# A 1-core fp32 transformer kernel: two matmuls per split product instead of three, down projections in two passes, four-block sums

## The reference

```python
# first block, D_FF = 2752
x = x + 0.5 * swiglu(rms_norm(x, ffn1_norm), w_gate, w_up, w_down)
u = rms_norm(x, mix_norm) @ w_in
x = x + concat([fourier_mixer(u[:, :512]), gqa_attention(q, k, v)]) @ w_out
x = x + 0.5 * swiglu(rms_norm(x, ffn2_norm), w_gate, w_up, w_down)
x = rms_norm(x, final_norm)
# second stack, D_FF = 2816
x = x + short_conv_mixer(rms_norm(x), w_in, w_conv, w_out)
x = x + mem_cross_attention(rms_norm(x), mem_n, w_q, w_kv, w_o)
x = x + swiglu(rms_norm(x), w_gu, w_down)
x = x + moba_attention(rms_norm(x), w_q, w_o, ..., shared_kv(x))
x = x + mem_cross_attention(rms_norm(x), ...)
x = x + swiglu(rms_norm(x), w_gu, w_down)
return rms_norm(x)
```

## Time and profile before

| | |
|---|---|
| median of 3 runs | 1349.37 us (1345.59, 1349.37, 1350.83) |
| profiled execution: span from first to last instruction | 1344.9 us |
| its own time | not listed apart; the nearest run is 1345.59 us |
| TensorE matmuls busy | 1296.3 us, 96%, 10402 records |
| weight loads busy | 1277.9 us, 95% |
| VectorE, ScalarE, POOL busy | 823.6, 588.4, 117.2 us |
| mean granted TensorE clock | 0.984 of full speed |
| read from HBM | 218.47 MB, 163 GB/s over the span |

### The profile page before, as it was taken

One profiled execution on the slowest core, in us unless ns is written; L12 is line 12 of the kernel. 1 busy time (PEld: TensorE's weight loads), 2 busy tenths in 40 slices (PEclk: granted clock), 3 DMA queues, 4 the chain that ended last, 5 costly groups with the idle time before them and its releaser, 6 DMA issues.

```text
span 1344.9 us, 25191 instructions
## 1 busy us (share of the span) xinstructions
PE 1296.3 (96%) x10402; PEld 1277.9 (95%) x10402; DVE 823.6 (61%) x1137; ACT 588.4 (44%) x717; POOL 117.2 (9%) x67
## 2 busy tenths in 40 slices
PE   7999999999999999999999999998999999999997
PEld 7999999889999999999999999998999999999997
DVE  7766745666666746876555666556966546566633
ACT  6544433454444434344434444443445335444432
POOL 2100002002000000002002000016621001100000
PEclk9999998999999999999998999999999999999998
DMA  8555643234555653554344555544444344455540
GB/s 312 200 187 188 219 156 125 67 122 157 175 177 183 221 183 107 187 177 157 126 152 142 179 185 188 207 141 154 131 142 169 132 148 141 172 176 175 201 167 32
DMA packets 33540, 220.53 MB, mean 164 GB/s; under 512 B 3616, under 2 KB 4928, under 8 KB 7488
## 3 DMA queue, kind: packets, MB, share of 16 engines
q1 hardware_dynamic: 33328, 219.46, 47.8%
q10 hardware_dynamic: 144, 0.07, 0.0%
HBM read 218.47 MB, written 1.05 MB: 163 GB/s over the span
## 4 chain that ended last, share of the span: by engine, by line
PE 87%; POOL 6%; DVE 3%; ACT 2%; issue 1%; DMA 0%; SPq 0%; POOLq 0%; DVEq 0%; ACTq 0%
PE bank L366 27%; PE bank L368 27%; PE bank L367 27%; POOL work L355 4%; PE bank L581 2%; PE bank L545 1%; PE bank L426 1%; ACT work L718 1%; DVE w_lo L933 1%; POOL q_t L344 1%; DVE x L955 1%; PE bank L563 0%; ACT xn_hi L714 0%; PE bank L436 0%; POOL q_t L347 0%
## 5 line engine op out<-in xcount | busy, mean ns | idle before, releaser
L705 ACT ACTIVATE w_hi<-raw 128x2048 fp32r<-128x2048 f32 x202 | 386.6, 1914 | 415.1 <-PE bank L368 411.6
L366 PE MATMUL bank<-xn_hi,w_hi 128*128 128x256 f32 x1856 | 534.7, 288 | 7.6 <-DVE xn_lo L943 7.3
L368 PE MATMUL bank<-xn_hi,w_lo 128*128 128x256 f32 x1856 | 531.4, 286 | 0.0
L367 PE MATMUL bank<-xn_lo,w_hi 128*128 128x256 f32 x1856 | 531.3, 286 | 0.0
L933 DVE TENSOR_TENSOR w_lo<-raw,w_hi 128x2048 fp32r<-128x2048 f32 x202 | 463.9, 2297 | 101.9 <-ACT w_hi L705 101.8
L366 PEld LDWEIGHTS bank<-xn_hi,w_hi 128*128 128x128 f32 x1856 | 362.9, 196 | 8.7 <-DVE xn_lo L943 7.8
L367 PEld LDWEIGHTS bank<-xn_lo,w_hi 128*128 128x128 f32 x1856 | 362.9, 196 | 0.1
L368 PEld LDWEIGHTS bank<-xn_hi,w_lo 128*128 128x128 f32 x1856 | 362.6, 195 | 0.0
L366 PE MATMUL bank<-h_hi,w_hi 128*128 (+1 forms) x1088 | 312.5, 287 | 0.9 <-DVE h_lo L1287 0.7
L367 PE MATMUL bank<-h_lo,w_hi 128*128 (+1 forms) x1088 | 307.8, 283 | 0.0
L368 PE MATMUL bank<-h_hi,w_lo 128*128 (+1 forms) x1088 | 307.7, 283 | 0.0
(11 more groups left out here) (158 smaller groups left out, 1095.1 us busy)
## 6 DMA issues: line engine op xcount, KB each, us to landing
raw<-weights SPq DMA_DIRECT2D x202, 1024.0 KB, 4.9
raw<-weights SPq DMA_DIRECT2D x4, 512.0 KB, 8.0
raw<-weights SPq DMA_DIRECT2D x4, 256.0 KB, 5.5
x<-x_t SPq DMA_DIRECT2D x4, 256.0 KB, 5.9
mem<-mem_t SPq DMA_DIRECT2D x1, 1024.0 KB, 8.9
out_t<-work SPq DMA_DIRECT2D x4, 256.0 KB, 2.2
v_s<-fourier SPq DMA_DIRECT2D x2, 256.0 KB, 5.2
con<-consts SPq DMA_DIRECT2D x1, 385.5 KB, 8.4
```

The costliest lines, as they stand in the source:

```text
L366: pe.matmul(out, hi, rhs_hi, start=first, stop=False, skip_group_check=True)
L367: pe.matmul(out, hi, rhs_lo, start=False, stop=False, skip_group_check=True)
L368: return pe.matmul(out, lo, rhs_hi, start=False, stop=last, skip_group_check=True)
L705: act.activation(w_hi[slot][:], raw[slot][:], ACT.Copy).then_inc(weight_hi, 1)
```

## The change

- A product is two matmuls. High and low part of an activation lie side by side (`xn`, `mn`, `h` are [128, blocks, 2, 256]), and w_hi takes both in one matmul of 512 columns; w_lo takes the high part in one of 256, into the second half of the same bank. `value_tile` does the same with the weights moving.
- An output block fills a whole bank (two halves, to be added), a tile a pair of banks. The table PAIRS gives each tile one of four pairs A, B, C, DD; `stat` is the last bank of DD, attention uses C and DD. ScalarE copies the second halves to `rest_s` (three buffers), VectorE adds the first halves and then multiplies by r_x, in SBUF.
- A down projection has two passes of 4 output blocks over the 22 blocks of h. A raw slot is filled by two transfers of 512 KB, one for each half tile. The first two output pairs are added to x while the second pass runs.
- Sums: POOL makes two additions of pairs (1 and 2 to 0); TensorE sums blocks 0, 1, 6 and 7, 8 matmuls, earlier in the next stage's second tile; the spread stands in the same tile.
- The convolution's first tap goes to ScalarE, the scaling of x and of the taps to POOL, the factor of z is the square `r_2`. Moba's query pair 0 is rotated on VectorE. The memory input shares the tile `k_t` and is read from HBM a second time. The hardware loops of all queues are written out.

```diff
-            def products(out, hi, lo, rhs_hi, rhs_lo, first, last):
-                pe.matmul(out, hi, rhs_hi, start=first, stop=False, skip_group_check=True)
-                pe.matmul(out, hi, rhs_lo, start=False, stop=False, skip_group_check=True)
-                return pe.matmul(out, lo, rhs_hi, start=False, stop=last, skip_group_check=True)
+            def product(out, hi, lo, a, first, last):
+                pe.matmul(out, hi, a.rearrange("p a s -> p (a s)"), start=first, stop=False, skip_group_check=True)
+                return pe.matmul(out[:, S:2 * S], lo, a[:, 0, :], start=False, stop=last, skip_group_check=True)
...
-                blocks, cols = (1, 1) if name in FOLD else (KB, 2) if name == "mix0" else (KB, 1)
+                blocks = [0, 1, 6, 7] if name in FOLD else list(range(KB))
...
-            def norm(name, late=False):
-                return {1: {7 if late else 4: lambda: sums(name)}, 2: {5 if late else 3: lambda: spread_factor(name)}}
+            def norm(name, start=False):
+                if start:
+                    return {1: {7: lambda: sums(name)}, 2: {5: lambda: spread_factor(name)}}
+                return {1: {1: lambda: sums(name), 7: lambda: spread_factor(name)}}
...
+                    for half, (d, u) in enumerate(DOWN_HALVES[2 * i:2 * i + 2]):
+                        if u == 0:
+                            if d:
+                                pe.wait_ge(spread_taken, SUM[norm_name] + 1)
+                            emptied(name, 2 * d)
+                            emptied(name, 2 * d + 1)
...
+                        for k in (2 * u, 2 * u + 1):
+                            for m in range(4):
+                                mm = block_of(i, half, d, k, m)
...
+            def rest(name, j, col=None, factors=0):
+                i, src = ROT[name] + j, pair_banks(name, j)[:, :, S:2 * S]
+                act.wait_ge(tile_done, FIRST[name] + j + 1)
...
+                    act.activation(rest_s[i % 3][:], src, ACT.Copy).then_inc(rest_copied, 1)
...
+                out = pair_banks(write, b)
+                link(dve.scalar_tensor_tensor(x[:, pair(b), :], out[:, :, S:2 * S], scale, x[:, pair(b), :], ALU.mult, ALU.add))
+                dve.scalar_tensor_tensor(x[:, pair(b), :], out[:, :, 0:S], scale, x[:, pair(b), :], ALU.mult, ALU.add).then_inc(added, 1)
...
+            def whole_of(name, j, dst, told=None):
+                i = ROT[name] + j
+                dve.wait_ge(rest_copied, i + 1)
+                e = dve.tensor_tensor(dst, pair_banks(name, j)[:, :, 0:S], rest_s[i % 3][:], ALU.add)
...
+            def scaled(name, j, dst, r):
+                whole_of(name, j, dst)
+                dve.tensor_tensor(dst, dst, both(r), ALU.mult).then_inc(drained, 1)
...
+            def conv():
+                pool.wait_ge(spread_taken, SUM["mix0"] + 1)
+                for p in range(KP):
+                    for k in (2 * p, 2 * p + 1):
+                        pool.tensor_scalar(x[:, k, :], x[:, k, :], v("final_norm", k), None, ALU.mult).then_inc(x_scaled, 1)
...
+                    pool.tensor_tensor(x[:, pair(p), :], x[:, pair(p), :], both(r_1[:]), ALU.mult).then_inc(x_scaled, 1)
+                    pool.wait_ge(tap_whole, 2 * (p + 1))
+                    pool.tensor_tensor(tap_s, tap_s, both(r_x[:]), ALU.mult).then_inc(tap_scaled, 1)
```

More of the change, by code:

```diff
@@ L780, in exponentials, with pieces @@
                     e.then_inc(a_exp, 1)
+                def pieces(n, i):
+                    for j in ended(kind, n, i):
+                        rest_part(kind, j)
+                        after(FIRST[kind] + j)
                 exponentials(0)
@@ L787, in attention @@
                     if n == 0:
-                        for j in ended(kind, n, 0):
-                            after(FIRST[kind] + j)
+                        pieces(n, 0)
                     act.wait_ge(a_turned, u + 1)
@@ L898, in _ @@
             after(FIRST["mem1"] - 1)
-            for j in range(AHEAD["mem1"] - 1):
-                after(FIRST["mem1"] + j)
+            ahead("mem1")
             attention("mem1")
```

859 lines of the change are left out of this document (470 added, 389 removed).

## The result

The changed kernel takes 1328.74 us (median of four runs, 1326.24 to 1330.95), the kernel before 1350.1 us beside it: a ratio of 0.9842, 95% interval 0.9821 to 0.9864. That is 21 us faster, where 91 were forecast. The profiled execution of the changed kernel took 1330.95 us, its span is 1328.9, so the two profiled spans lie only 16 us apart.

The account below looks back on a forecast made before the run. TensorE's own pace, the three matmuls of a product, was taken as the bound. From a span of 1344.9 us, -78.3 (products), -18.8 (sums) and +6 (evictions, smaller edits) gave 1253.8, with 4.5 for the runs' median 1258 us; range 1230 to 1305.

Parts of the forecast that it names:

- Part 1: TensorE products: two matmuls in place of three, 0.336 us instead of 0.360 for each of 3264, -78.3 us.
- rival A: Products: a fixed 0.013 us per fp32r matmul whatever its length, 0.347 us a product, 1293 us; chance 0.20.
- rival B: Products: the 0.013 us grows with the columns, so only 10 us are saved, 1326 us; chance 0.11.
- Part 2: Four-block sums: 20.5 us of waits go, 10 us of clock come back, 11.7 us of records are added; -18.8 us.
- rival E: Sums still wait or their one-column matmuls let the clock fall: +20 us, 1278 us; chance 0.52 together with the forecast.
- Part 3: Two-step evictions of product tiles: hidden in gate-up tiles, VectorE busy 4.25 of 5.38 us; attention charged +3 us.
- rival D: Gate-up tiles: evictions become the bound on ScalarE, 7.0 us a tile, about 1399 us; chance 0.07.
- Part 4: Smaller edits: moba rotation -3 us, convolution 4 us, down projections 0, output ends +1, tail +1.
- The cover: The tile of matmuls and three pairs of banks hide gate-up evictions at no cost; wrong if new TensorE waits exceed 25 us.
- main step: The saving from two matmuls per product, 0.336 us each; wrong if the pair of starts exceeds 0.345 us.

Follow-up runs that it names:

- m1_columns: Kernel of TensorE matmul stretches alone, by length and type; fp32r starts every 0.120 us for 256 columns, 0.227 for 512, 0.174 for 384.
- b_four: The kernel before with the four-block sums alone (two additions on POOL, 8 matmuls); 1339.56 us, ratio 0.9912.
- d_query: The changed kernel with the last two query heads of moba's causal attention turned on VectorE instead of GpSimd; 1322.6 us, ratio 0.9821.

## Why the prediction was wrong

**Part 1, the step that failed.** The term 0.216 + 0.120 = 0.336 us. Measured: 0.227 + 0.120 alone, 0.350 on average in the kernel, so 32.6 us instead of 78.3. The step behind it read "the rest does not scale with the columns in clocks; it is a floor of about 0.12 us for one load and one matmul". The observation at 1.2 GHz was right and still holds, in the changed kernel too (timeline of PE behind the wait at 544 us):

```profile
547.46 0.63 PE L396 MATMUL bank<-xn,wt 128*128 128x512 f32 x1
...
548.10 0.63 PE L396 MATMUL bank<-xn,wt 128*128 128x512 f32 x1
```

0.64 us a pair is 768 bare columns. But that 0.013 us vanishes at the lower clock doesn't make it a floor at the higher one: 256, 384 and 512 columns in m1_columns all carry it. The Trainium skill (TensorE: Matmul & The Clock Gate, Wait — 56ns, not 53.3ns?) describes just this, a fixed cost of each matmul that shows only at 2.4 GHz; the runs agree on both halves, and only its size is another in fp32r. The nearest row by cycles was an fp32 stream; of the nearest by type, the fp32r matmul itself, there was only one length, and to say what a second length costs it has to be read as rival A or as rival B. Rival A gave 1293 us; with the second pace (0.0033 us more on average, 11 us), 8 us less from the sums and 18 more of waits its sum is 1330. So rival A had the mechanism and B the number. Rival B's time, 1326, is the closest, by accident: its mechanism, 0.013 us that grow with the columns, is refuted by m1_columns.

**Part 2.** Right in its places: no wait of TensorE at the sums, 208 records of them. The size was -10.5 us for -18.8 in both kernels that show the sums alone: some 5 us for the clock instead of 10, since rival E was partly true, and in b_four 4.2 us of waits that stay. That new waits bring drops of their own was put at nothing; in the changed kernel they took most of the clock's gain back.

**Part 3.** Right for the gate-up tiles: VectorE is busy 5.55 - 1.26 = 4.29 us a tile, 4.25 were put; rival D did not appear. Wrong in the ends: before a down projection the half tile of 2.8 us covers a chain of 4.3 (0.60 + 0.69 + 0.69 + 2.28) us, and a wait of 1.57 us comes twice. Attention was charged 3 us. Its waits for values, for moba's query, for the normalising, for h and for the exponentials come to 20.3 us (4.7 + 6.9 + 3.8 + 3.7 + 1.2) and 1.2 of smaller ones, against 10.5 before. A copy on ScalarE is 0.6 us; what it costs is its place in two queues.

**Part 4.** Moba: forecast -3 for the waits on GpSimd's rotation, and they are 6.9 us for 7.1, now in one wait of 6.2; the whole stage went from 108.5 to 111.9 us. Convolution: forecast +4, and conv_in grew by 2.5 us in spite of a pace worth some 2 us there: right. Down projections: rightly free.

**The cover.** The text said that the forecast is wrong in its main step if the pair of starts is over 0.345 us, and in its cover if new waits exceed 25 us. It is 0.350, so the main step failed by its own sign, and the new waits are 24 us, at that edge. Of the 70 us between forecast and result, the product's term is 46, the sums 8, and the cover some 18.

## What to carry to other kernels

A matmul merged away is worth its fixed cost only, and that cost is read from the same data type at a second length: where no row has the length that the change introduces, the forecast should stay with the rows of its own type rather than with those of equal cycles. An eviction in two steps on two engines is paid for in the queues: in the steady tiles it was free, and where tiles are short or the engines take turns, the copy belongs ahead of whatever the tensor engine doesn't wait for, and behind what it does. A wait of 2.3 us was followed by 3.4 us at half clock in 12 of 16 places and one of 1.4 us, in the same places, in none of 8, so shaving a wait can be worth three times its length. A change that removes waits in one place and opens others gets the clock back in the first and can lose it in the second.

## What the runs showed of the hardware that was not expected

- fp32r at 2.4 GHz: 13.3 ns a matmul beside the columns at 256, 320, 384 and 512, 16 ns at 448; bf16 2.5 ns. At 1.2 GHz the fp32r pair takes the bare columns, 0.64 us.
- A run of fp32r pairs of 512 and 256 columns locks at its start into 0.3467 or 0.353 us a pair, with TensorE alone: both after waits equal to 3 ns, the faster one in all five stretches behind gaps up to 0.80 us. In the order 512, 512, 256, 256 the changed kernel's long stretches had a single pace, 0.3483 us. With 320 in place of 256 it took 0.380 each time, 0.0066 over the sum of the two alone.
- VectorE is held by GpSimd as well as the other way round. Two operations of 128x128 in d_query, beside GpSimd's multiplications of 32x512 (3.23 and 1.28 us from 959.48 on) and without them (timeline of DVE):

```profile
962.00 2.11 DVE L1184 TENSOR_SCALAR scratch<-scratch,small 128x128 f32<-128x128 f32 x2
...
973.77 0.55 DVE L1184 TENSOR_SCALAR scratch<-scratch,small 128x128 f32<-128x128 f32 x2
```

2.11 and 0.55 us. That is the other half of the price of work on GpSimd, and the attention's probabilities wait behind it.
